# Score matmuls of the fine decay levels: four 32 by 32 squares on the diagonal in place of one 128 by 128 block

## The chip, the cores and the metric

The kernel runs on one core of a Trainium2 chip. The metric is the device time of one execution in microseconds (us), as the median of several executions of the same program. One profiled execution comes with it. It has a span, the time from the first instruction to the last, and a time of its own that is a little longer.

The engines are TensorE (PE in the rows, with its weight loads listed apart as PEld), VectorE (DVE), ScalarE (ACT), GpSimd (POOL) and SyncE (SP), which issues DMAs here. Each works through its own list of instructions in order. They wait for each other through semaphores.

## What is computed

The reference is one layer of a hybrid encoder over 1,024 frames of width 2,048: a norm, one large projection, three groups of heads, gates, an output projection, a residual and a final norm. The change touches group A alone, six gated linear recurrences with a state of 128 by 128:

```python
def hgrn2_group(q, f_logit, i, lb, gain):
    ...
    def step(state, inp):
        qn, kn, vn, gn = inp
        b = jnp.cumsum(gn, axis=2)
        b_last = b[:, :, -1:, :]
        o_inter = jnp.einsum('bhtk,bhkv->bhtv', qn * jnp.exp(b), state)
        diff = b[:, :, :, None, :] - b[:, :, None, :, :]
        decay = jnp.exp(jnp.where(causal[:, :, None], diff, -jnp.inf))
        scores = jnp.einsum('bhtsk,bhsk->bhts', qn[:, :, :, None, :] * decay, kn)
        o = o_inter + jnp.einsum('bhts,bhsv->bhtv', scores, vn)
    ...
```

The score of frames t and s within a chunk carries a decay of its own for every one of the 128 channels, exp(b_t - b_s). A plain product of two matrices can't give that without dividing by tiny numbers, and the kernel gets around it by levels.

## The kernel before

**Blocks and levels.** The kernel cuts the 1,024 frames into 8 blocks of 128 (`BLK` is 8, `P` is 128) and works with causal scores inside a block. `LEVELS` is 64, 32, 16, 8, 4, 2, 1. At level `size`, a block of 128 falls into groups of 2 x `size` frames. The pairs that count have s in the early half of a group and t in the late half. Both decays are then taken against the last frame of the early half, so that every exponent is at most zero: VectorE writes an operand LV in which late columns hold q times a decay and early columns k times a decay. One product of LV with itself, contracted over the 128 channels, has the wanted scores in the squares "early against late", and things nobody wants elsewhere. Level 1 (neighbours) goes another way (`near` in the code), so six levels, n = 0 to 5 (sizes 64 to 2), go through `a_level(u, n)` for each head u.

**What TensorE does at a level.** For n = 0 and 1 (`n < WIDE`) it computes only the squares that count: per block one of 64 by 64 (n = 0), or two of 32 by 32 (n = 1), which land on output partitions 0 to 31 and 64 to 95. For n = 2 to 5 the squares that count are smaller than 32, and it computes the whole 128 by 128 product of the block at line 862. That makes 8 matmuls for each of four levels and six heads, 192 in all. Operands are plain float32. The profile shows each such matmul as two records of MATMUL, with two weight loads, and therefore x16 for 8 blocks. The scores go to one of two PSUM tiles, `mix[n % 2]`.

**What VectorE does.** `lv_diff_of` (lines 1770 and 1771) and `lv_mult` (lines 1777 and 1779) build LV for a level; ScalarE takes the exponential in between (line 1119). `lv_ready` is raised by line 1779. `lv_drain` takes the scores out of PSUM into the matrix SC: for n = 0, 1 by a plain copy of the squares, for n = 2 to 5 by `copy_predicated` (line 1828) of all 128 by 1,024 elements under an int8 mask `level` that is one only in the squares that count. What stands outside them in PSUM never reaches SC.

**What sets the order.** TensorE's list is written out by hand. Its main work in this part is the projection (`project`, line 799): for every output tile 16 slices of 128 channels, each by three products of float32 halves (hi x hi, lo x hi, hi x lo) and two halves of 512 frames, 6 matmuls of 128 x 512 a slice. After every second slice (12 matmuls) comes a slot, `stages[...]`, in which a piece of some head's work may stand. Head u of group A begins at slot b = -4 + 20 u. `a_diag_level` (with level 0) stands at b + 8, levels 1 to 5 at b + 9, 11, 12, 13 and 15, `a_near` at b + 16, the transposes at b + 17, the state at b + 18, the output at b + 20, and sums of squares (lines 829 and 830) at b + 22 and b + 24. A stage waits for its data (`lv_ready`, `parts_split`) and for its PSUM tile to be drained (`fill`). TensorE's list does not move on while it waits.

**Weights.** SyncE loads float32 weights, 256 KB at a time, into one of four slots. GpSimd splits them into `w_hi` (line 751) and `w_lo` (line 753), and TensorE releases the slot after 24 matmuls (`w_used`).

Of the kernel before, what the change touches and what calls it, by code (L numbers as in the profile page):

```python
# [37 lines left out]
P = 128  # L38
# [53 lines left out]
NL = len(LEVELS)  # L92
NM = NL - 1
WIDE = 2


A_M0, A_M1 = 6, 7
# [9 lines left out]
def shape_tables():  # L107

    t = np.arange(P)
    ident = np.eye(P, dtype=np.float32)  # L110
    level = np.zeros((P, NL - WIDE, P), np.float32)
    for n, size in enumerate(LEVELS[WIDE:]):
        same = (t[:, None] // (2 * size)) == (t[None, :] // (2 * size))
# [20 lines left out]
def build(nc, xT, wi, w, wo, gain, lbl, hgain, relb, fgain, ident_d, level_d, start_d, rot_d, dec_d, outT):  # L134
# [4 lines left out]
    with ExitStack() as ctx:  # L139
        def sb(name, shape, dt=F32):  # L140
            return ctx.enter_context(nc.sbuf_tensor(name, shape, dt))
# [5 lines left out]
        def next_at():  # L147
            return (nc.sbuf_base + 31) // 32 * 32

        def over(name, shape, offset, dt=F32):  # L150
# [3 lines left out]
        at = next_at()  # L154
# [32 lines left out]
                   for m in range(IN_RAWS)]  # L187
        level = sb("level", [P, NL - WIDE, P], I8)
        gain_sb = sb("gain_sb", [P, KB])
# [17 lines left out]
        def blocks(n):  # L207
            return arena[:, n, :].rearrange("p (c t) -> p c t", c=BLK)
# [6 lines left out]
        CQK, CK, CQD, CSC, CST, CKT, CCOS, CSIN, CDEC = Q, K, B, LV0, LV1, SC, ST, KDT, QE  # L215
        level_f32 = arena[:, SC, 0:(NL - WIDE) * P].rearrange("p (l t) -> p l t", l=NL - WIDE)
        start_f32 = arena[:, Q, 0:HALF]
        relrow = arena[0:B_HEADS, Q, HALF:HALF + REL]
        rel_wide_row = arena[0:B_HEADS, T3, 0:BAND + P]
        LV = [LV0, LV1]  # L220
# [45 lines left out]
        def mixb(n):  # L266
            return mix[n][:, :].rearrange("p (c t) -> p c t", c=BLK)
# [497 lines left out]
        def _(pe):  # L765
# [42 lines left out]
            def fill(n, before):  # L808

                if not (isinstance(before, int) and before == 0):  # L810
                    pe.wait_ge(drained[n], before)
# [35 lines left out]
            def a_level(u, n):  # L847
                def stage():
                    m = n % 2
                    pe.wait_ge(lv_ready, 2 * (NM * u + n + 1))  # L850
                    fill(m, (A_M0 * u + n // 2) if m == 0 else (A_M1 * u + 1 + n // 2))
                    size = LEVELS[n]
                    for c in range(BLK):
                        if n < WIDE:
                            for early in range(0, P, 2 * size):
                                late = early + size
                                last = nc.tensor.matmul(
                                    mixb(m)[early:early + size, c, late:late + size],
                                    blocks(LV[n % 2])[:, c, early:early + size],
                                    blocks(LV[n % 2])[:, c, late:late + size], start=True, stop=True)  # L860
                        else:
                            last = nc.tensor.matmul(mixb(m)[:, c, :], blocks(LV[n % 2])[:, c, :],  # L862
                                                    blocks(LV[n % 2])[:, c, :], start=True, stop=True)
                    last.then_inc(filled[m], 1)
                return stage

# [741 lines left out]
        def _(dve):  # L1608
# [192 lines left out]
            def near_drain(u):  # L1801
# [5 lines left out]
                odd = blocks(SC).rearrange("p c (t two) -> p c t two", two=2)[:, :, :, 1]  # L1807
                mask = level[:, NM - WIDE:NM - WIDE + 1, 1::2].to_broadcast([P, BLK, P // 2])
                nc.vector.copy_predicated(odd, mask, mix[0][:, 0:HALF].rearrange(
# [500 lines left out]
```

## Time and profile before

| | us |
|---|---|
| median of 3 runs | 1829.19 |
| lowest and highest of them | 1824.94, 1829.94 |
| the profiled execution, own time | 1832.73 |
| its span | 1830.9 |
| PE busy in it | 1780.6 |
| DVE busy | 1215.3 |
| POOL busy | 769.6 |
| ACT busy | 667.0 |

A matmul's recorded duration includes its way through the array, and so records overlap: a row of the time line with "x16" spans from the first start to the last end. What one matmul costs the engine is the distance between starts, and this comes from such a row as (span minus one duration) / (count minus one). The heads of group A have their levels between 607 and 1003 us of the span.

### The profile page before, as it was taken

What the parts mean: (1) busy time and instruction counts of PE and PEld (TensorE: products, weight loads), DVE (VectorE), ACT (ScalarE), POOL (GpSimd) and SP (SyncE); (2) the same over time, 40 slices, a digit from 0 to 9 for tenths busy, and PEclk for the clock granted to TensorE, in tenths of its full rate; (3) what the DMA queues carried; (4) which work ended last, traced back from release to release, by engine and by line L of the source; (5) the groups of instructions that cost most, each with busy time, mean ns of one, the idle gap of its engine ahead of it and who ended that gap; (6) DMA issues with size and microseconds to landing.
All of it is one profiled execution on the core that took longest, in us unless ns stands there. A gap on an engine that the chain in (4) does not pass through costs nothing.

```text
span 1830.9 us, 23721 instructions
## 1 busy us (share of the span) xinstructions
PE 1780.6 (97%) x8758; PEld 1473.3 (80%) x8758; DVE 1215.3 (66%) x1704; ACT 667.0 (36%) x974; POOL 769.6 (42%) x545
## 2 busy tenths in 40 slices
PE   7999999999999999999999999999999999999996
PEld 6888888888887788888888777777888877888874
DVE  7756666464778987877887245445654457777877
ACT  4433434342434344343343223322543223333442
POOL 4544444444455443444434323333334350355541
PEclk9999999999999999999999999999999999999998
DMA  7777778685987223233223332233333369578875
GB/s 249 228 229 250 254 220 275 205 282 167 316 288 225 90 96 104 75 104 93 87 81 114 101 105 86 87 94 122 115 116 95 112 216 352 183 244 262 282 236 220
DMA packets 160838, 323.08 MB, mean 176 GB/s; under 512 B 18378, under 2 KB 19151, under 8 KB 160724
## 3 DMA queue, kind: packets, MB, share of 16 engines
q1 hardware_dynamic: 146458, 276.52, 47.3%
q10 hardware_dynamic: 14266, 45.05, 7.2%
q8 instruction: 70, 1.15, 0.3%
q14 instruction: 44, 0.36, 0.1%
HBM read 275.35 MB, written 46.15 MB: 176 GB/s over the span
## 4 chain that ended last, share of the span: by engine, by line
PE 88%; DVE 7%; DMA 2%; issue 1%; ACT 1%; POOL 1%; SPq 1%; DVEq 0%; ACTq 0%; POOLq 0%
PE prj L799 33%; PE prj L778 29%; PE prj L1078 12%; PE mix L862 2%; PE mix L934 2%; PE mix L917 2%; PE mix L818 1%; DMA y_in<-y_scratch 1%; DVE arena L2246 1%; PE mix L927 1%; PE mix L889 1%; DVE mv_lo L1734 1%; PE mix L892 1%; PE mix L878 1%; DVE w_lo L2191 1%
## 5 line engine op out<-in xcount | busy, mean ns | idle before, releaser
L751 POOL TENSOR_SCALAR w_hi<-w_sum 128x512 fp32r<-128x512 f32 x124 | 202.4, 1632 | 550.0 <-DMA w_sum<-in_w 532.0
L778 PE MATMUL prj<-in_hi,w_hi 128*128 128x512 f32 x840 | 329.7, 392 | 9.9 <-DVE w_lo L1668 8.8
L778 PE MATMUL prj<-in_lo,w_hi 128*128 128x512 f32 x840 | 328.4, 391 | 0.0
L778 PE MATMUL prj<-in_hi,w_lo 128*128 128x512 f32 x840 | 328.2, 391 | 0.0
L799 PE MATMUL prj<-mv_hi,w_hi 128*128 128x512 f32 x928 | 300.0, 404 | 2.5 <-issue 2.5
L738 POOL TENSOR_TENSOR w_sum<-in_raw,in_raw 128x512 f32<-128x512 f32 x150 | 200.8, 1339 | 212.9 <-PE prj L778 201.9
L799 PE MATMUL prj<-mv_lo,w_hi 128*128 128x512 f32 x928 | 288.4, 392 | 0.0
L799 PE MATMUL prj<-mv_hi,w_lo 128*128 128x512 f32 x928 | 287.2, 391 | 0.0
L799 PEld LDWEIGHTS prj<-mv_lo,w_hi 128*128 128x128 f32 x928 | 174.9, 188 | 38.3
L799 PEld LDWEIGHTS prj<-mv_hi,w_lo 128*128 128x128 f32 x928 | 174.7, 188 | 38.4
L778 PEld LDWEIGHTS prj<-in_hi,w_hi 128*128 128x128 f32 x840 | 158.5, 189 | 44.3 <-issue 9.2
L799 PEld LDWEIGHTS prj<-mv_hi,w_hi 128*128 128x128 f32 x928 | 165.3, 189 | 31.3 <-issue 3.7
L1668 DVE TENSOR_TENSOR w_lo<-w_sum,w_hi 128x512 fp32r<-128x512 f32 x150 | 115.5, 771 | 110.1 <-ACT w_hi L1181 106.1
L1078 PE MATMUL prj<-mv_hi,w_hi 128*128 128x512 f32 x448 | 176.6, 394 | 9.6 <-DVE mv_lo L2209 5.3
L778 PEld LDWEIGHTS prj<-in_lo,w_hi 128*128 128x128 f32 x840 | 158.7, 189 | 33.4 <-issue 0.5
L778 PEld LDWEIGHTS prj<-in_hi,w_lo 128*128 128x128 f32 x840 | 158.6, 189 | 33.3
L760 POOL TENSOR_TENSOR raws<-raws 128x512 f32<-128x512 f32 x80 | 113.5, 1419 | 170.6 <-DMA raws<-in_wo 170.6
L1119 ACT ACTIVATE arena<-arena 128x1024 f32<-128x1024 f32 (+1 forms) x121 | 123.5, 1033 | 144.2 <-DVE arena L1771 119.3
L1078 PE MATMUL prj<-mv_hi,w_lo 128*128 128x512 f32 x448 | 175.7, 392 | 0.0
L1078 PE MATMUL prj<-mv_lo,w_hi 128*128 128x512 f32 x448 | 175.6, 392 | 0.0
L753 POOL TENSOR_TENSOR w_lo<-w_sum,w_hi 128x512 fp32r<-128x512 f32 x124 | 170.9, 1378 | 10.3
L1181 ACT ACTIVATE w_hi<-w_sum 128x512 fp32r<-128x512 f32 x150 | 94.2, 628 | 175.0 <-POOL w_sum L738 174.7
(173 smaller groups left out, 2548.9 us busy)
## 6 DMA issues: line engine op xcount, KB each, us to landing
in_raw<-in_wi SPq DMA_DIRECT2D x360, 256.0 KB, 3.3
raws<-in_wo SPq DMA_DIRECT2D x184, 256.0 KB, 3.7
w_sum<-in_w SPq DMA_DIRECT2D x116, 256.0 KB, 3.2
arena<-z_scratch ACTq DMA_DIRECT2D x56, 512.0 KB, 3.9
y_in<-y_scratch SPq DMA_DIRECT2D x80, 256.0 KB, 4.6
z_scratch<-acc_in SPq DMA_DIRECT2D x60, 256.0 KB, 3.9
z_scratch<-stage SPq DMA_DIRECT2D x26, 512.0 KB, 4.1
x_even<-in_xT SPq DMA_DIRECT2D x44, 256.0 KB, 4.0
```

Source lines behind the costliest of these rows:

```text
L738: nc.gpsimd.tensor_tensor(w_sum[wslot(n)][:], in_raw_buf(a), in_raw_buf(b), ALU.add if sign > 0 else ALU.subtract).then_inc(in_wsum, 1)
L751: nc.gpsimd.tensor_scalar(w_hi[q][:], w_sum[q][:], 1.0, None, ALU.mult).then_inc(w_hi_done, 1)
L753: nc.gpsimd.tensor_tensor(w_lo[q][:], w_sum[q][:], w_hi[q][:].bitcast(F32), ALU.subtract).then_inc(w_split, 1)
L760: nc.gpsimd.tensor_tensor(raw_buf(a), raw_buf(a), raw_buf(b), ALU.add if sign > 0 else ALU.subtract).then_inc(wsum_done, 1)
L778: last = nc.tensor.matmul(out, wt[wslot(n)][:, i % GRAN, :], mv[j % 2][:, i, :], start=(i == 0 and wt is w_hi and mv is in_hi), stop=(i == ...
L799: last = nc.tensor.matmul(prj[pair][:, half(side)], wt[wslot(q)][:, kk, :], mv[:, k, half(side)], start=(k == 0 and wt is w_hi and mv is m ...
L862: last = nc.tensor.matmul(mixb(m)[:, c, :], blocks(LV[n % 2])[:, c, :], blocks(LV[n % 2])[:, c, :], start=True, stop=True)
L917: last = nc.tensor.matmul(mix[0][:, lo:hi], blocks(BQ)[:, p, :], arr(BK)[:, first * P + lo:first * P + hi], start=True, stop=True)
L1078: last = nc.tensor.matmul(bank(s), wt[wslot(W0 + n)][:, i % GRAN, :], slot(mv, j, i), start=(i == 0 and wt is w_hi and mv is mv_hi), stop= ...
L1119: return nc.scalar.activation(out, src, ACT.Exp, **kw)
L1181: nc.scalar.activation(w_hi[wslot(n)][:], src, ACT.Copy).then_inc(in_w_hi, 1)
L1668: tt(w_lo[wslot(n)][:], src, w_hi[wslot(n)][:].bitcast(F32), ALU.subtract).then_inc(w_split, 1)
```

## The change

For levels n = 2 to 5 the one matmul of 128 by 128 per block becomes four of 32 by 32: stationary and moving operand are both the same 32 columns of LV (all 128 channels), and the output is the square on the diagonal, on output partitions 0, 32, 64 or 96 onwards. A group of 2 x `size` frames, at most 32, lies inside such a square. The draining `copy_predicated` still reads the whole tile under the mask.

```diff
+ROWS = 32
...
                         else:
-                            last = nc.tensor.matmul(mixb(m)[:, c, :], blocks(LV[n % 2])[:, c, :],
-                                                    blocks(LV[n % 2])[:, c, :], start=True, stop=True)
+                            for at in range(0, P, ROWS):
+                                part = blocks(LV[n % 2])[:, c, at:at + ROWS]
+                                last = nc.tensor.matmul(mixb(m)[at:at + ROWS, c, at:at + ROWS], part, part,
+                                                        start=True, stop=True)
                     last.then_inc(filled[m], 1)
```

TensorE's list before, around level 2 of head 0 (`prj` is the projection's accumulator in PSUM, `mix` the scores, `arena` holds LV; "64x64" and the like are the output):

```order
L799 MATMUL prj<-mv_hi,w_hi 128x512
L799 MATMUL prj<-mv_lo,w_hi 128x512 x2
L799 MATMUL prj<-mv_hi,w_lo 128x512 x2
L862 MATMUL mix<-arena 128x128 [waits mix0_drained,lv_ready]
L862 MATMUL mix<-arena 128x128 x7
L799 MATMUL prj<-mv_hi,w_hi 128x512 [waits w_split,in_acc_done]
```

The same place after:

```order
L800 MATMUL prj<-mv_hi,w_hi 128x512
L800 MATMUL prj<-mv_lo,w_hi 128x512 x2
L800 MATMUL prj<-mv_hi,w_lo 128x512 x2
L865 MATMUL mix<-arena 32x32 [waits mix0_drained,lv_ready]
L865 MATMUL mix<-arena 32x32 x31
L800 MATMUL prj<-mv_hi,w_hi 128x512 [waits w_split,in_acc_done]
```

Eight matmuls became 32 in the same place, behind the same waits; nothing else on TensorE or on another engine moved.

## Rows read from the trace of the kernel before

**Rows 1.** The page: busy us (share of the span) and instructions by engine
```profile
span 1830.9 us, 23721 instructions
...
PE 1780.6 (97%) x8758; PEld 1473.3 (80%) x8758; DVE 1215.3 (66%) x1704; ACT 667.0 (36%) x974; POOL 769.6 (42%) x545
```

**Rows 2.** PE's groups from 614 to 1002 us: count | busy, mean ns | idle
```profile
L799 PE MATMUL prj<-mv_hi,w_hi 128*128 128x512 f32 x426 | 136.1, 401 | 0.0
...
L862 PE MATMUL mix<-arena 128*128 128x128 f32 x384 | 46.7, 275 | 0.0
```

**Rows 3.** Two head periods: length, busy of PE, PEld, DVE, ACT, POOL, granted clock, DMA
```profile
614.00:687.00 73.00, 73.00 (x428) 62.30 (x424) 60.10 (x74) 29.97 (x34) 31.84 (x21) 1.00 0.26 79
687.00:760.00 73.00, 73.00 (x424) 62.28 (x425) 58.47 (x72) 29.75 (x33) 29.67 (x20) 1.00 0.31 96
```

**Rows 4.** Chain of work that ended last, 614 to 690 us: start, us, what
```profile
630.58 5.46 PE prj L799 x24
636.04 1.78 PE mix L862 x16
637.82 2.73 PE prj L799 x12
```

**Rows 5.** Time line of PE in head 0: start, us, what
```profile
619.14 0.61 PE L799 MATMUL prj<-mv_hi,w_lo 128*128 128x512 f32 x2
619.60 1.95 PE L862 MATMUL mix<-arena 128*128 128x128 f32 x16
621.30 0.71 PE L799 MATMUL prj<-mv_hi,w_hi 128*128 128x512 f32 x2
621.84 0.62 PE L799 MATMUL prj<-mv_lo,w_hi 128*128 128x512 f32 x2
...
628.64 1.95 PE L862 MATMUL mix<-arena 128*128 128x128 f32 x16
...
640.39 0.39 PE L829 MATMUL mix<-part_hi,ones 128*128 128x512 f32 x1
```

**Rows 6.** Time line of PE around level 1 of head 1
```profile
685.65 0.61 PE L799 MATMUL prj<-mv_hi,w_lo 128*128 128x512 f32 x2
686.19 0.70 PE L857 MATMUL mix<-arena 128*32 128x32 f32 x32
686.82 0.73 PE L799 MATMUL prj<-mv_hi,w_hi 128*128 128x512 f32 x2
687.39 0.40 PE L799 MATMUL prj<-mv_lo,w_hi 128*128 128x512 f32 x1
```

**Rows 7.** PE, middle of a group of each shape (windows of under 1 us)
```profile
620.04 1.39 PE L862 MATMUL mix<-arena 128*128 128x128 f32 x11
...
682.51 0.81 PE L857 MATMUL mix<-arena 128*64 128x64 f32 x11
...
686.28 0.61 PE L857 MATMUL mix<-arena 128*32 128x32 f32 x28
```

**Rows 8.** PE's groups of line 857: count | busy, mean ns | idle before
```profile
L857 PE MATMUL mix<-arena 128*64 128x64 f32 x96 | 6.9, 225 | 0.0
L857 PE MATMUL mix<-arena 128*32 128x32 f32 x192 | 4.2, 197 | 1.5 <-DVE arena L1908 1.5
```

**Rows 9.** Level 1 of head 0, the one that begins after a wait
```profile
613.39 0.70 PE L857 MATMUL mix<-arena 128*32 128x32 f32 x32 [1.47 <-DVE arena L1908]
```

**Rows 10.** Time line of DVE in head 0: operands of level 4, part sums
```profile
626.46 0.68 DVE L1779 TENSOR_TENSOR arena<-arena 128x512 f32<-128x512 f32 x1
...
637.12 0.69 DVE L1799 TENSOR_TENSOR part_lo<-arena,part_hi 128x512 fp32r<-128x512 f32 x1
```

**Rows 11.** Time line of DVE in head 1
```profile
694.38 0.69 DVE L1770 TENSOR_TENSOR arena<-arena 128x512 f32<-128x512 f32 x1 [2.23 <-PE mix L862]
...
697.52 1.79 DVE L1779 TENSOR_TENSOR arena<-arena 128x512 f32<-128x512 f32 x1
...
709.62 0.68 DVE L1799 TENSOR_TENSOR part_lo<-arena,part_hi 128x512 fp32r<-128x512 f32 x1
```

**Rows 12.** Time line of PE in head 1: level 4, near level
```profile
701.44 1.95 PE L862 MATMUL mix<-arena 128*128 128x128 f32 x16
...
713.20 0.39 PE L829 MATMUL mix<-part_hi,ones 128*128 128x512 f32 x1
```

**Rows 13.** Page: fetches of instructions; POOL's weight split; DMA issues of weights
```profile
q8 instruction: 70, 1.15, 0.3%
...
L751 POOL TENSOR_SCALAR w_hi<-w_sum 128x512 fp32r<-128x512 f32 x124 | 202.4, 1632 | 550.0 <-DMA w_sum<-in_w 532.0
...
L753 POOL TENSOR_TENSOR w_lo<-w_sum,w_hi 128x512 fp32r<-128x512 f32 x124 | 170.9, 1378 | 10.3
...
w_sum<-in_w SPq DMA_DIRECT2D x116, 256.0 KB, 3.2
```

## The prediction

> **What bounds the kernel now.** I began with the busy shares. TensorE is busy 1780.6 of 1830.9 us, VectorE 66% and the others under half [rows 1]. A share over the whole span says nothing of one stage, so I then took TensorE's groups in the stretch that holds the levels, 614 to 1002 us. Its idle time ahead of the projection and ahead of line 862 is 0.0 [rows 2]. In two periods of a head, 73.00 us each, TensorE is busy all 73.00 us and VectorE 60.10 and 58.47 [rows 3]. The chain that ended last goes through projection, line 862, projection, with nothing between [rows 4]. There the reader should see that each group of line 862 stands bare on the path with 1.78 us. All 24 groups are alike (384 records are 24 x 16 [rows 2]). Whatever TensorE gains in them comes off the end, so long as nobody else is late.
>
> **What a group costs now.** From the start of the last projection row before it to the second row after it, 619.14 to 621.84, are 2.70 us [rows 5]. Four projection records lie in that; twelve take 2.73 us [rows 4], thus 0.2275 each, 0.91 together. The group costs 2.70 - 0.91 = 1.79 us. Within it starts are (1.39 - 0.275) / 10 = 111.5 ns apart [rows 7, 2]. So 15 distances are 1.67 and the fixed part is 0.12 us.
>
> **What 32 by 32 matmuls cost.** Level 1 already runs such matmuls, 16 of them (32 records), from the same operand type into the same PSUM tiles [rows 6]. By the same sum, 685.65 to 687.39 is 1.74, less 0.91, or 0.83 us. The distance of starts is (0.61 - 0.197) / 27 = 15.3 ns in the middle of a group [rows 7, 8] and (0.70 - 0.197) / 31 = 16.2 ns over a whole one [rows 6]. I take 15.8. The fixed part is 0.83 - 31 x 0.0158 = 0.34 us, more than the 0.12 of full blocks: going over to small tiles and back costs 0.22 us a group.
>
> 15.8 ns is less than the size alone gives. 128 columns cost 111.5 ns and 64 columns (0.81 - 0.225) / 10 = 58.5 [rows 7, 8]. A straight line through both gives 32.0 ns for 32 columns, and level 1 runs at half of that. The 64-column squares of level 0 all land on the same output partitions, while level 1 alternates between partitions 0 to 31 and 64 to 95. I read this as two records under way at once when their output partitions differ.
>
> **The change, term by term.** It takes away 8 full matmuls a group and adds 32 small ones, 64 records, in the same slot behind the same waits. The cost of a group is 0.34 + 63 x d, where d is the distance of starts. It breaks even at d = (1.79 - 0.34) / 63 = 23.0 ns. The one unknown is d, since no row shows four neighbouring tiles in turn. Its bounds from rows are 8.0 ns below (four tiles at once, a quarter of 32.0) and 32.0 above (no overlap).
>
> I take 15.8. Each float32 matmul is two records on one tile, one after the other. If matmuls start in program order, the second of a square and the first of the next square can run together, but not the two of one square. That gives two at once with two tiles and with four alike. A group then costs 0.34 + 63 x 0.0158 = 1.34 us, 0.45 less than now, and 24 groups save **10.8 us**.
>
> The Trainium skill speaks against this change: "TensorE: Matmul & The Clock Gate", section "Wait — 56ns, not 53.3ns?", has start-to-start never under about 25 ns however few the columns. By that floor a group would cost 1.92 us and 24 of them 3.0 us more than now. This trace disagrees with it, with 15.3 to 16.2 ns at level 1 [rows 6, 7].
>
> **Who is late next.** TensorE reaches each later stage of a head 0.45 us sooner per level passed, 1.8 us by the near level. The tightest places are in head 0. Level 4 starts at 628.64 [rows 5], would start 0.91 sooner at 627.73, and its operand is ready at 626.46 + 0.68 = 627.14 [rows 10]: 0.6 left. The near level starts at 640.39, would start at 638.57, and its parts are ready at 637.81 [rows 5, 10]: 0.8 left. In head 1, level 4 starts at 701.44 [rows 12], would at 700.53, and is ready at 699.31 [rows 11]. The near level starts at 713.20, would at 711.38, and is ready at 710.30 [rows 11, 12]. VectorE itself waits 2.23 us for line 862 there and also moves forward [rows 11]. I count no new wait. Were this cover gone, head 0 alone would lose some tenths of a us. VectorE's work is unchanged: it would be busy 60.10 of some 71.2 us in a head's period.
>
> The drains are the same instructions, and `filled` comes sooner, so they cost nothing. Weights: a slot is refilled in 3.2 + 1.6 + 1.4 = 6.2 us [rows 13], while TensorE works through the other three in 3 x 24 x 0.2275 = 16.4 us. The cover is 10 us and the change takes at most 1 us of it. What follows group A (attention, retention, output) is held to TensorE's list by the same semaphores and starts 10.8 us sooner; I find no fixed date in it.
>
> Instructions: 48 more matmul records and as many weight loads a group, 2,304 in all, 13% more of TensorE's 17,516 [rows 1]. They come from memory, 1.15 MB in 70 packets [rows 13], so some nine more packets, which no engine waits for by itself. The burst could outrun the supply. At level 1 of head 0, TensorE had waited 1.47 us and still ran 32 records in 0.70 us [rows 9], the same as from a full queue [rows 6]. That shows the rate for 32 records in a row, not for 64. I price it at nothing and leave it a small chance.
>
> **The rivals.**
>
> *Four at once.* If each tile keeps its own queue, d is 8.0 ns, a group costs 0.34 + 0.50 = 0.84, and 24 save 22.8 us. Then head 0 waits: level 4 would start at 626.74 against 627.14 ready (0.4 lost), and the near level at 636.99 against 637.81 (0.8 lost). Net 21.6 us: 1807.6. For it: tiles are independent, and level 1 can't tell this case from mine. Against it: with two tiles under way at level 1 and program order kept, the second record of a square blocks everything behind it. The Trainium skill supports this rival in "TensorE: Matmul & The Clock Gate", section "Part 3: Packing small matmuls — row/col tiling": matmuls on different tiles start some 4 ns apart; the same section has them start and end strictly in program order, which supports my reading. Chance 0.14.
>
> *Overlap only across the halves.* Level 1's tiles lie in different halves of the output. If 0 to 31 and 32 to 63 can't overlap, six steps of 32.0 carry eight records and d is 24.0. A group costs 1.85, 24 of them 1.4 us more: 1830.6. Nothing in the rows speaks for it, but no row shows neighbours. Chance 0.11, any d from 22 to 26 included. The 25 ns of the Trainium skill's page above would lie in this case, at 1832.2.
>
> *Slower: no overlap at all.* Every change of tile is now to a neighbour (and from the last one back to the first). If this needs the tile before to finish, d is 32.0 and a group costs 2.36: 0.57 more, 13.7 us in all, 1842.9. It decides from d = 23.0 upwards. Against it is level 1, where a change of tile overlaps well. Chance 0.08.
>
> *Others.* The supply of instructions gives out in the burst, or TensorE's granted clock, 1.00 (2.4 GHz) through these stretches [rows 3], falls to 1.2 GHz because small tiles work it less. Level 1's bursts didn't do that, but they are half as long. Either costs more than it leaves. Chance 0.05, slower.
>
> **How the numbers follow.** My case has 0.62. The profiled span becomes 1830.9 - 10.8 = 1820.1 and its own time 1832.7 - 10.8 = 1821.9. The profiled run lies 3.5 us above the median, so I take the difference off the median: 1829.2 - 10.8 = **1818.4**. Runs before spread from 1824.9 to 1829.9, so this case covers about 1813 to 1823 by itself. The range should hold the four-at-once case with some of that spread (1806) and the overlap across halves with as much (1832). It leaves out 0.13 of slower cases and some tails. A measurement of this kernel tells about 0.3%, 5.5 us, from no change. Faster by more than that: nearly all of my case and all of four at once, 0.73. Within it: 0.14. Slower: 0.13.
>
> **What would show it.** Line 865 should have 1,536 records of 128*32, groups of 64 that span about 63 x 0.0158 + 0.197 = 1.19 us. A span of 0.7 us is four at once; 1.7 is the half overlap; 2.2 is none. In the chain a group should weigh about 1.3 instead of 1.78. A head's period should be 1.8 us shorter, about 71.0 instead of 72.8. TensorE's idle time in 604 to 1000 us should stay near nothing; new waits for lines 1779 or 1799 in head 0 would mean that VectorE took some back. The forecast fails if d isn't 15.8, if the granted clock drops, or if the 10.8 us reappear as TensorE's idle time behind 1003 us.

## The result and the profile after

The changed kernel takes 1811.71 us as the median of 6 runs (1807.45 to 1813.21). The kernel before took 1829.57 beside it (6 runs, 1824.94 to 1834.99). The medians differ by 17.9 us. The ratio of the runs is 0.9893, with a 95% interval from 0.9877 to 0.9909; times 1829.57 that is 19.6 us less, between 16.7 and 22.5. Forecast were 10.8 us less. The direction was right; the size was near that of the rival with four tiles at once.

The page of the changed kernel, busy us by engine and instruction fetches:

```profile
span 1807.3 us, 26025 instructions
...
PE 1754.1 (97%) x9910; PEld 1438.8 (80%) x9910; DVE 1218.9 (67%) x1704; ACT 666.7 (37%) x974; POOL 772.3 (43%) x545
...
q8 instruction: 79, 1.29, 0.3%
```

Against [rows 1] the span fell by 23.6 us and TensorE's busy time by 26.5. There are 1,152 more matmul records (576 more matmuls) and 1,152 more weight loads, 2,304 in all, and nine more packets of instructions [rows 13].

TensorE's groups by shape: count | busy us, mean ns | idle before:

```profile
L865 PE MATMUL mix<-arena 128*32 128x32 f32 x1536 | 18.3, 199 | 0.2 <-DVE arena L1782 0.2
L858 PE MATMUL mix<-arena 128*64 128x64 f32 x96 | 6.9, 225 | 0.0
L858 PE MATMUL mix<-arena 128*32 128x32 f32 x192 | 4.2, 197 | 1.5 <-DVE arena L1911 1.5
```

Levels 2 to 5 were 46.7 us busy [rows 2] and are 18.3; levels 0 and 1 are as they were [rows 8].

The time line of TensorE around level 2 of head 1, the counterpart of [rows 5] (start, us, what):

```profile
688.23 0.61 PE L800 MATMUL prj<-mv_hi,w_lo 128*128 128x512 f32 x2
688.78 0.76 PE L865 MATMUL mix<-arena 128*32 128x32 f32 x64
689.47 0.73 PE L800 MATMUL prj<-mv_hi,w_hi 128*128 128x512 f32 x2
690.04 0.62 PE L800 MATMUL prj<-mv_lo,w_hi 128*128 128x512 f32 x2
```

The reader should see that 64 records span 0.76 us, hardly more than the 0.70 of 32 records at level 1 [rows 6]. Starts are (0.76 - 0.199) / 63 = 8.9 ns apart. By the sum of the prediction the group costs 690.04 - 688.23 - 0.91 = 0.90 us, and it cost 1.79: 0.89 saved.

The gain can be read off exactly in the period of a head, from level 0 of one head to level 0 of the next. It was 72.80 us before. Two periods after (length, busy us of PE, PEld, DVE, ACT, POOL, granted clock, DMA):

```profile
678.46:747.66 69.20, 69.20 (x615) 57.28 (x614) 57.30 (x71) 29.85 (x33) 32.09 (x21) 1.00 0.30 97
747.66:816.86 69.20, 69.20 (x615) 57.27 (x614) 57.06 (x71) 28.83 (x32) 31.47 (x20) 1.00 0.30 95
```

Both ends of each window are starts of a level 0. The period is 69.20 us, 3.60 less, or 0.90 for each of four levels. TensorE is still busy without a break and its granted clock is still 1.00 (2.4 GHz). Heads 0 to 4 give 2.9 + 4 x 3.60 and the four levels of head 5 another 3.6: 20.9 us in the profiled execution. Another 0.8 us of the 23.6 had come before the first level, where nothing is changed. The last 1.9 us lie behind the last level, and most of them have nothing to do with the change. In the trace of before, TensorE waits 2.00 us at 1051.16, and its next wait of this kind comes 33.11 us later:

```profile
1051.16 0.41 PE L927 MATMUL mix<-ident,arena 128*128 128x128 f32 x2 [2.00 <-DVE arena L2034]
...
1084.27 0.74 PE L927 MATMUL mix<-ident,arena 128*128 128x128 f32 x5 [0.47 <-DVE arena L2034]
```

The trace of after has the first wait too (2.07 us, at 1029.58), and the second 31.50 us later:

```profile
1061.08 0.74 PE L930 MATMUL mix<-ident,arena 128*128 128x128 f32 x5 [0.48 <-DVE arena L2037]
```

The same work between the two took 1.6 us longer before, because the granted clock was 0.67 in the 4 us from the end of the first wait, partly the lower of its two levels (1.2 GHz), and 0.92 in the next 5 (4 x 0.33 + 5 x 0.08 = 1.7), where the first profile of after has 1.00. This comes and goes: two further profiles of the changed kernel, shown below, have 0.61 and 0.57 in the 4 us behind that wait. The 20.9 us in the heads agree with the 19.6 us of the timed runs.

### The profile page after: what moved, and what is told of

Same layout as the page of the kernel before. It is cut to its first block, busy times and chain, and to the rows that moved or that the text cites. A ratio compares the mean times of both kernels' runs of the same rounds, so it can differ in the third digit from the quotient of the medians.

```text
span 1807.3 us, 26025 instructions
## 1 busy us (share of the span) xinstructions
PE 1754.1 (97%) x9910; PEld 1438.8 (80%) x9910; DVE 1218.9 (67%) x1704; ACT 666.7 (37%) x974; POOL 772.3 (43%) x545
## 4 chain that ended last, share of the span: by engine, by line
PE 84%; DVE 8%; DMA 3%; issue 2%; ACT 1%; SPq 1%; POOL 1%; DVEq 0%; ACTq 0%; POOLq 0%
PE prj L800 33%; PE prj L779 29%; PE prj L1081 11%; DMA y_in<-y_scratch 2%; PE mix L937 2%; PE mix L920 2%; PE mix L819 1%; DVE arena L2249 1%; PE mix L930 1%; PE mix L865 1%; DVE w_lo L2194 1%; PE mix L892 1%; DVE arena L2224 1%; DVE mv_lo L1737 1%; PE mix L830 1%
## 5 line engine op out<-in xcount | busy, mean ns | idle before, releaser
L752 POOL TENSOR_SCALAR w_hi<-w_sum 128x512 fp32r<-128x512 f32 x124 | 206.6, 1666 | 521.3 <-DMA w_sum<-in_w 503.5
L1671 DVE TENSOR_TENSOR w_lo<-w_sum,w_hi 128x512 fp32r<-128x512 f32 x150 | 119.8, 803 | 106.9 <-ACT w_hi L1184 105.1
```

What stands on the lines that cost most here:

```text
L752: nc.gpsimd.tensor_scalar(w_hi[q][:], w_sum[q][:], 1.0, None, ALU.mult).then_inc(w_hi_done, 1)
L1671: tt(w_lo[wslot(n)][:], src, w_hi[wslot(n)][:].bitcast(F32), ALU.subtract).then_inc(w_split, 1)
```

## The experiments

Theory A: a matmul occupies the range of 32 output partitions that it writes, for 32 ns a record with 32 moving columns. Ranges work side by side, all four of them, and a record that must wait for its range doesn't stop the next few behind it. Theory B: small matmuls are cheap by themselves, or TensorE picks freely from its queue, and neither order nor range matters. The changed kernel alone fits both. The period of a head serves as the measure, since within a run it repeats to 0.04 us where TensorE waits for nothing, and it is 69.20 us in all three profiles of the changed kernel. The cost of a group is 0.90 + (period - 69.20) / 4.

### One range after the other

```diff
-                            for at in range(0, P, ROWS):
+                        for c, at in [(c, at) for at in range(0, P, ROWS) for c in range(BLK)]:
```

> The same 32 squares per level, in another order: all 8 blocks on output partitions 0 to 31, then all on 32 to 63, and so on. Theory A (each range of 32 output partitions works through its own matmuls one after another at 32 ns a record, up to four ranges side by side, and TensorE looks ahead at most a few matmuls): with 16 records in a row for one range, nothing runs side by side but at three changes; starts are near 32 ns apart, a group costs 0.34 + 63 x 0.031 = about 2.3 us instead of 0.90, a head's period is 69.2 + 4 x 1.4 = 74.8 us, and the time is about 12 us above the kernel before (1842). Theory B (small tiles are cheap by themselves, or TensorE picks freely among all that is queued): the order makes no difference, 69.2 us a period, 1811.

Measured: 1839.78 us (8 runs) against 1830.13, ratio 1.0050 [1.0037, 1.0063]. The same 32 squares in another order take back the whole gain and more. Time line of TensorE, level 2 of head 1 and the two starts of level 0 that give the period:

```profile
684.65 1.15 PE L862 MATMUL mix<-arena 128*64 128x64 f32 x16
...
694.97 1.91 PE L857 MATMUL mix<-arena 128*32 128x32 f32 x64
...
758.52 1.15 PE L862 MATMUL mix<-arena 128*64 128x64 f32 x16
```

(The diff shows the order against the changed kernel. Line numbers differ: here 857 stands for the changed levels and 862 for levels 0 and 1.) The period is 73.87 us and a group costs 2.07. Starts are (1.91 - 0.199) / 63 = 27.2 ns apart, where strictly one after another would give 32. So at each of three changes of range some records did overlap. Theory B falls. Theory A stands, with a short reach ahead: 63 distances of 32.0 ns are 2.02 us and took 1.71, and the 0.31 us that were hidden, shared among three changes, are 0.10 us or some 3 records at each. The single starts of this group show it directly. The second comes 52 ns after the first, and then they follow each other every 32 ns up to the 13th, at 400 ns. The last three of the first range follow at 432, 464 and 494 ns, and in front of each stands another start, at 406, 458 and 490. I take these three for the next range's, since behind 494 the distance is 32 ns again. The other two changes look alike.

### Two ranges in turn, far and near

```diff
+                        for c, at in [(c, at) for pair in ((0, 64), (32, 96)) for c in range(BLK) for at in pair]:
```

> The same squares, two ranges of output partitions in turn: 0 and 64 for all blocks, then 32 and 96. Theory A (a range is busy 32 ns a record; k ranges in turn give 32/k): starts 16 ns apart as at level 1, a group costs 0.34 + 63 x 0.0158 = 1.34 us, a head's period 69.2 + 4 x 0.44 = 71.0 us, 1811 + 10.6 = 1822. Theory B (any two small tiles side by side are as good as four): 69.2 us, 1811.

Measured: 1819.21 us (4 runs), ratio 0.9936 [0.9917, 0.9956].

```profile
679.05 1.15 PE L862 MATMUL mix<-arena 128*64 128x64 f32 x16
...
689.37 1.11 PE L857 MATMUL mix<-arena 128*32 128x32 f32 x64
...
749.72 1.15 PE L862 MATMUL mix<-arena 128*64 128x64 f32 x16
```

The period is 70.67, a group costs 1.27 and starts are (1.11 - 0.199) / 63 = 14.5 ns apart, half of 32 less some overlap where the pair changes. Theory A had said 71.0. This is about what the prediction took for the changed kernel, and it is what the kernel would do if only two ranges could be under way.

The neighbours variant has `((0, 32), (64, 96))` in the same place.

> As the run with two far ranges in turn, but with neighbours: 0 and 32, then 64 and 96. Theory A (ranges don't disturb each other wherever they lie): the same 71.0 us a head as with far ones. Rival (neighbours share a path): starts nearer to 32 ns, up to 2.3 us a group and 74.8 us a head.

Measured, one run: 1821.84 us. The starts of level 0 are 680.17 and 750.84:

```profile
680.17 1.03 PE L862 MATMUL mix<-arena 128*64 128x64 f32 x14
...
750.84 1.15 PE L862 MATMUL mix<-arena 128*64 128x64 f32 x16
```

The period is 70.67 us, the same to the last digit. Neighbouring ranges don't disturb each other. (The view was cut off at 681 us, hence x14 and 1.03.)

### Two squares of 64 by 64

```diff
-ROWS = 32
+ROWS = 64
```

> One size changed: two squares of 64 by 64 on the diagonal for each block instead of four of 32 by 32. Theory A: a record of 64 columns holds its 64 output partitions for 58.5 ns, two in turn give 29.2 ns; a group of 32 records costs 0.34 + 31 x 0.0292 = 1.25 us, a head's period 69.2 + 4 x 0.35 = 70.6 us, 1811 + 8.4 = 1819. Rival (64-wide tiles don't run side by side): 0.34 + 31 x 0.0585 = 2.15 us, 74.2 us a head, 1841.

Measured: 1819.53 us (4 runs), ratio 0.9945 [0.9924, 0.9966].

```profile
680.05 1.15 PE L858 MATMUL mix<-arena 128*64 128x64 f32 x16
...
690.36 1.15 PE L865 MATMUL mix<-arena 128*64 128x64 f32 x32
...
750.88 1.15 PE L858 MATMUL mix<-arena 128*64 128x64 f32 x16
```

The two shapes to compare stand in one kernel. Line 858 writes one range of 64 partitions with every matmul, and 16 records span 1.15 us. Line 865 alternates between two ranges, and 32 records span 1.15 us. The period is 70.83 and a group costs 1.31; expected were 70.6 and 1.25. Overlap isn't a property of 32-wide tiles.

### Two blocks in a row on each range

```diff
+                        for c, at in [(c, at) for c0 in range(0, BLK, 2) for at in range(0, P, ROWS) for c in (c0, c0 + 1)]:
```

> The same squares, each range of 32 output partitions now gets two blocks (four records) in a row before the next range. Theory A (one record at a time per range at 32 ns, program order kept, and a small number of records may be waiting ahead). In the run with 16 records in a row some 2.6 of each 16 were hidden (63 x 0.027 = 1.70 us against 2.02): with the same reach each four cost 1.4 x 32 = 45 ns, starts are about 11 ns apart, a group costs 1.04 us and a head's period is 69.8 us. If only one record may wait per range, each four cost 71 ns, starts are 18 ns apart, a group costs 1.46 us, a period is 71.4 us. If the engine looks far ahead: 69.2 us.

Measured, one run: 1813.28 us.

```profile
678.63 1.15 PE L862 MATMUL mix<-arena 128*64 128x64 f32 x16
...
688.94 0.86 PE L857 MATMUL mix<-arena 128*32 128x32 f32 x64
...
748.33 1.15 PE L862 MATMUL mix<-arena 128*64 128x64 f32 x16
```

The period is 69.70 and a group costs 1.03, against 69.8 and 1.04 from the reach that the first experiment had shown. The mean distance is (0.86 - 0.199) / 63 = 10.5 ns. That only one record may wait per range (71.4) is out, and so is a long reach (69.2).

### Level 0 in two ranges

```diff
+                                for at in range(early, early + size, ROWS):
+                                    last = nc.tensor.matmul(
+                                        mixb(m)[at:at + ROWS, c, late:late + size],
+                                        blocks(LV[n % 2])[:, c, at:at + ROWS],
...
```

> Level 0 alone changed: its square of 64 by 64 as two matmuls of 32 output partitions by 64 columns, 32 records a group instead of 16. Theory A (a range is busy for its moving columns, 58.5 ns for 64): two ranges in turn give 29.2 ns, 32 records cost what 16 cost at 58.5 ns, a head's period stays at 69.2 us within 0.05. Rival (a matmul with fewer output partitions is cheaper by itself): level 0 costs up to 0.45 us less, 68.75 us a period.

Measured, one run: 1812.78 us.

```profile
679.90 1.09 PE L859 MATMUL mix<-arena 128*32 128x64 f32 x32
...
749.16 1.09 PE L859 MATMUL mix<-arena 128*32 128x64 f32 x32
```

The period between these starts is 69.26 us, 0.01 more than the expectation allowed, and in later heads 69.22, against 69.20. Twice as many records of half as many output partitions cost the same to 0.06 us: a range is busy for its moving columns, and nothing is gained by a narrower output with as many columns. That a matmul with fewer output partitions is cheaper by itself (68.75 us) is out.

### Two levels behind each other

```diff
-                put(b + 12, a_level(u, 3))
+                put(b + (12 if u == 0 else 11), a_level(u, 3))
```

> The changed kernel with level 3 of heads 1 to 5 moved one slot forward, right behind level 2. Two groups of small matmuls then share one change from full blocks to small tiles and back. If the fixed part of a group (0.35 us) is this change, each of five heads gains about 0.3 us, a period is 68.9 us instead of 69.2, and the time is 1.5 us below the changed kernel, which timing hardly resolves. If the fixed part belongs to each group by itself, nothing is gained. Level 3's operand was ready 3.8 to 5.0 us before its old place and 3.6 us are taken, so a wait of some tenths may come in.

Measured: 1811.30 us (5 runs), ratio 0.9890 [0.9871, 0.9908]; the changed kernel beside it (next run) has 0.9903 [0.9886, 0.9921]. The times don't tell them apart.

```profile
679.86 1.15 PE L858 MATMUL mix<-arena 128*64 128x64 f32 x16
...
690.17 1.36 PE L865 MATMUL mix<-arena 128*32 128x32 f32 x128
...
748.78 1.15 PE L858 MATMUL mix<-arena 128*64 128x64 f32 x16
```

The trace does: the period is 68.92 us, 0.28 less. So most of a group's fixed 0.34 us is the passage from full blocks to small tiles and back, and two groups that stand together pay it once. The Trainium skill says in "TensorEngine Tiling (Array Packing)", section "Key Properties", that a change of tiling mode drains TensorE. By that the second group would be free of it, and the trace agrees.

### The changed kernel again, and VectorE's order

> The changed kernel again, for the comparison on the same chip: 69.20 us a head's period, 0.989 of the kernel before.

Measured: 1814.82 us (5 runs), ratio 0.9903 [0.9886, 0.9921]. Its periods are 69.20 but for head 3 (70.51), and head 0 is 1.0 us longer than in the first profile (72.44 against 71.42). In both places TensorE waits at the near level (1.12 us in head 0, 1.02 in head 3). First TensorE at the near level of head 3, in the first profile of the changed kernel and with VectorE's operand for it:

```profile
841.87 1.78 DVE L1802 TENSOR_TENSOR part_lo<-arena,part_hi 128x512 fp32r<-128x512 f32 x1
...
844.28 0.39 PE L830 MATMUL mix<-part_hi,ones 128*128 128x512 f32 x1
```

Then the same place in the repeated run:

```profile
843.35 1.73 DVE L1795 TENSOR_TENSOR arena<-arena 128x512 f32<-128x512 f32 x1 [0.78 <-ACT arena L1122]
...
846.87 1.10 DVE L1802 TENSOR_TENSOR part_lo<-arena,part_hi 128x512 fp32r<-128x512 f32 x1
...
848.11 0.47 PE L830 MATMUL mix<-part_hi,ones 128*128 128x512 f32 x1 [1.02 <-DVE part_lo L1802]
```

Before the change this operand was ready 2.6 to 2.9 us ahead (in head 1: 709.62 + 0.68 against 713.20 [rows 11, 12]). In the first profile after it, it is 844.28 - (841.87 + 1.78) = 0.63 us in head 3, and 0.15 to 0.43 in the others. So little cover is used up when VectorE's instructions take longer than usual. Line 1795 took 0.69 us in the first profile and 1.73 here, but that isn't what made head 3 late. From its start to the end of line 1802 VectorE needed 4.55 us in the first profile (839.10 to 843.65) and 4.62 here. It had been late before: the head's level 0 came 2.65 us later on this trace's scale (819.51 against 816.86), line 1795 came 4.25 later. The 1.6 us between were lost in the levels ahead, at line 1773 (1.22 us at 830.63, 0.69 in the first profile) and line 1774 (1.78 us at 835.92, against 0.68). Why the same instruction takes 0.68 us in one place and 1.1 to 1.8 in another isn't shown.

The last version has levels 2 and 3 joined, and two steps exchanged on VectorE:

```diff
                         near_mult(u)
-                            silu_finish(2 * u + 1, GATE, 1.0)
                             part_low(arr(LV0)[:, 0:HALF], A_PARTS * u + 2)
+                            silu_finish(2 * u + 1, GATE, 1.0)
```

> The kernel with levels 2 and 3 joined, and on VectorE the low half of the near level's part sums (0.68 us) ahead of the gate's last step (1.22 us) instead of behind it. In the changed kernel the near level found its operand ready 0.15 to 0.64 us ahead, where it had been 2.6 to 2.9, and in the repeated run it waited 1.12 us in head 0 and 1.02 in head 3. If VectorE's order is what is late there, the near level's operand comes some 0.5 us sooner, and waits of that stage shrink: head 0 by 0.5, others to nothing; 0.5 to 1.5 us over the whole, against the joined kernel, hardly to be told in the times. If it isn't, the same waits remain.

Measured: 1809.48 us (4 runs) against 1832.28, ratio 0.9874 [0.9858, 0.9891].

> The changed kernel once more on the same chip as the run beside it: 0.989 to 0.990 of the kernel before, head periods of 69.20 us apart from waits at the near level.

Measured for the changed kernel beside it: 1812.35 us (4 runs), ratio 0.9891 [0.9875, 0.9907]. TensorE's idle time ahead of the part sums, over the whole kernel, in the joined kernel, in the last version, and in the changed kernel of this comparison:

```profile
L830 PE MATMUL mix<-part_hi,ones 128*128 128x512 f32 x40 | 16.3, 407 | 6.1 <-DVE part_lo L1802 6.1
```

```profile
L830 PE MATMUL mix<-part_hi,ones 128*128 128x512 f32 x40 | 16.1, 402 | 3.7 <-DVE part_lo L1802 3.7
```

```profile
L830 PE MATMUL mix<-part_hi,ones 128*128 128x512 f32 x40 | 16.2, 406 | 3.1 <-DVE part_lo L1802 3.0
```

These totals mix several stages. At the near level itself the joined kernel waits 1.11 us in head 0 and 0.27 in head 3, and the last version nowhere. The new order did bring the operand sooner: in heads 1, 2 and 4 it is ready 1.11, 1.00 and 0.99 us ahead, in the joined kernel 0.66, 0.79 and 0.60. But the changed kernel varies by as much by itself: its near level shows no wait in the first and the third profile, and for 2.1 us in the second. So the order's worth in time isn't shown. The last version is the fastest kernel tried, and 2.9 us below the changed one by the medians. The intervals overlap, so that isn't shown.

## Why the prediction was right, and where its size failed

**The number** lies in the stated range, 1806 to 1832, and the direction is right. But 1811.7 is 6.7 us under the 1818.4 of the main case, outside the 1813 to 1823 that this case covered. The range holds it because it was drawn wide enough for the rival with four at once.

**What bounds the kernel** held. TensorE is busy through every period of a head before and after, and 24 x 0.89 = 21.4 us saved in the groups became 20.9 us of span.

**The cost of a full group** (1.79 us) and **the sum 0.34 + 63 x d** held: with d = 8.9 ns it gives 0.90, as measured. Break-even at 23.0 ns held too. The run with two far ranges has 14.5 ns and is faster, the one with a range after the other has 27.2 and is slower.

**The term that was mis-sized is d**: 15.8 forecast, 8.9 measured. The step that failed is "the second record of a square blocks everything behind it". I had read level 1's rate as two records under way wherever, when it was two ranges in turn. Its rows can't tell these apart, and the text said so. The premise behind the step, that matmuls start in program order, doesn't hold for the starts of this trace. In level 2 of head 1 they come at 0, 6, 12 and 20 ns, then at 52, 58, 66 and 72, then at 84, 90, 96 and 104 (levels 3 of head 1 and 2 of head 2 run alike). A range takes one record per 32 ns, and a square's two records follow each other in the list; in strict order the second record of the first square would begin at 32 ns or later and hold up all behind it, so that one record alone could begin within the first 20 ns. I read the four as the first records of four squares, with the second ones waiting at their ranges. The run with 16 records in a row has this reach at some 3 records, and the second records of three squares are within it. The first round takes 52 ns instead of 32, and once in the middle some 20 ns slip; that is why the mean is 8.9 and not 8.0. Had I carried level 1's number as "32 divided by the ranges in turn", the sum would have been 0.84 us a group.

**The rival with four at once** is what happened. It had 0.84 us a group and 1807.6 us; measured were 0.90 and 1811.7. Its chance of 0.14 was too small for a case that the rows held as open as mine.

**Who is late next.** For that rival the text had waits in head 0 of 0.4 us at level 4 and 0.8 at the near level. Level 4 waits 0.2 (line 865 above). The near level of head 0 had no wait in the first profile, with 0.15 us left, and 1.1 us in the repeated one. The prediction left out that VectorE's own durations vary by a us from one execution to the next, so that 0.6 us of cover isn't cover in every execution. In the repeated profile heads 0 and 3 are longer by 1.02 and 1.31 us.

**No overlap, or only across the halves** are both out: near and far pairs gave 70.67 us alike. (The 1.4 us of the second are 1.5 by its own terms, 24 x (1.852 - 1.79).) **The supply of instructions** didn't give out: 64 records in 0.76 us, and 128 in 1.36 us in the joined kernel. The granted clock stayed at 1.00.

**The floor of 25 ns** from the start of one matmul to the next, in the Trainium skill's "TensorE: Matmul & The Clock Gate" (section "Wait — 56ns, not 53.3ns?"), would have made the kernel 3.0 us slower. The trace disagrees: 8.9 ns over 64 records. The 4 ns between different tiles of that page's section "Part 3: Packing small matmuls — row/col tiling" is nearer: within a round the trace has 6 to 8 ns between starts. But a round of four comes only every 32 ns, and this sets the 8.9, not the step between starts.

## What to carry to other kernels

When only squares on the diagonal of a product are wanted, compute these alone, and issue them so that consecutive matmuls write different ranges of 32 output partitions: the time is that of the moving columns through the busiest range. The order of the loops decided between 1.1% faster and 0.5% slower with the very same matmuls. Keep such groups together, since a group's passage from full to small tiles and back costs about 0.3 us. Look at how much cover the next waiting stage has left before taking more out of the bound engine.

## What the runs showed of the hardware

- In float32, a record with 32 moving columns holds its range of output partitions for 32 ns, one with 64 columns for 58.5 ns, at a granted clock of 1.00. Four ranges in turn gave 8.9 ns between starts, two gave 14.5 (and 29.8 with 64 columns), one 27.2 with overlap at its three changes and 32 ns between starts elsewhere.
- The number of output partitions didn't matter to a range's time: 32 by 64 in two ranges cost what 64 by 64 in one did (period 69.22 to 69.26 against 69.20 us).
- Overlap reaches past a blocked record by some 3 records: three starts of the next range stand among the last ones of the range before, and runs of two blocks on a range cost 1.03 us a group against 0.90 in rotation.
- A group that stands right behind another group of small tiles cost 0.28 us less than one that stands between full blocks (period 68.92 against 69.20 us).
- The granted clock was 0.57 to 0.67 in the 4 us behind a wait of some 2 us (line 927 before, 930 after) in some profiles, of the kernel before and of the changed one, and 1.00 there in others. In the trace of before, the work behind that wait took 1.6 us longer.
